# The causal mask of the first stage's attention, added by a product of identity and mask instead of by VectorE

## The reference

```
u = x @ w_in[l]                       # 1024 -> 7168 columns: conv, dq, dk, dv, mq, mk, mv, gates
y_a = conv_branch(...)                # depthwise causal convolution of 31 taps, layer norm, silu
# differential attention, 4 heads of two score matrices each:
s = einsum("qd,kd->qk", q, k) * scale
s = where(key_pos <= query_pos, s, -1e30)
p = softmax(s);  a = p[0] - lam * p[1];  o = a @ v
# moba attention, 8 heads: with 256 tokens and blocks of 256, plain causal attention
s = where(kpos <= qpos, s, -1e30);  p = softmax(s);  o = p @ v
m = gates[0] * y_a + gates[1] * y_b + gates[2] * y_c
x = layer_norm(ALPHA * x + m @ w_o[l])
h = relu(x @ w_ff1[l] + b)**2
x = layer_norm(ALPHA * x + h @ w_ff2[l] + b)
```

## Time and profile before

| | |
|---|---|
| time, median of 3 runs | 1386.25 us (1384.93 to 1388.49) |
| the profiled execution | 1385.95 us, span 1384.2 us |
| mean granted clock of TensorE | 0.975 |
| TensorE busy | 1293.9 us (93%), 8713 products |
| VectorE busy | 905.2 us (65%) |
| ScalarE busy | 586.5 us (42%) |
| mask adds (line 1216) | 32, of 428 ns each (median), from 85.2 to 650.8 us |
| score products (line 1903) | 64 in 128 passes of 272 to 480 ns, from 83.5 us on |

### The profile page before, as it was taken

How to read it: one execution, slowest core, us unless ns; L and a number is a source line. 1 busy time by engine, 2 the same in 40 slices (tenths; PEclk the granted TensorE clock), 3 DMA queues, 4 the chain that set the end, 5 groups by cost and what they waited for, 6 DMA issues and landing times.

```text
span 1384.2 us, 21687 instructions
## 1 busy us (share of the span) xinstructions
PE 1293.9 (93%) x8713; PEld 1096.8 (79%) x8713; DVE 905.2 (65%) x1464; ACT 586.5 (42%) x911; POOL 59.8 (4%) x84
## 2 busy tenths in 40 slices
PE   7999999989999899999898999969979979999996
PEld 6999888878888799999887888859878866555553
DVE  3999876876555789996587665684885573232223
ACT  3345674444444434566444444444535343111111
POOL 1000000000000000000000000020043000010100
PEclk9999999999999999999999999989999999999999
DMA  9754434565555456443355555555535576999994
GB/s 281 246 189 153 153 92 127 179 213 182 182 188 200 135 181 221 127 158 105 112 203 183 190 197 188 183 163 164 152 109 171 214 280 251 421 421 421 421 421 196
DMA packets 172583, 289.70 MB, mean 209 GB/s; under 512 B 10388, under 2 KB 143140, under 8 KB 160204
## 3 DMA queue, kind: packets, MB, share of 16 engines
q1 hardware_dynamic: 169580, 281.55, 58.1%
q0 software_dynamic: 2752, 6.82, 1.7%
q10 hardware_dynamic: 160, 0.08, 0.0%
HBM read 287.36 MB, written 3.16 MB: 210 GB/s over the span
## 4 chain that ended last, share of the span: by engine, by line
PE 64%; DVE 24%; ACT 5%; issue 3%; DMA 3%; SPq 1%; POOL 0%; DVEq 0%; ACTq 0%; POOLq 0%
PE ps L1775 11%; PE ps L1777 10%; PE ps L1776 10%; DVE w_lo L1144 8%; PE ps L1826 8%; PE ps L2272 7%; DVE cvh L1259 5%; ACT w_hi L737 4%; PE ps L1828 3%; PE ps L2304 3%; DMA raw<-in_w_up 2%; PE ps L2315 2%; DVE nm L1217 1%; DVE gT L1184 1%; DVE x_nat L1190 1%
## 5 line engine op out<-in xcount | busy, mean ns | idle before, releaser
L1144 DVE TENSOR_TENSOR w_lo<-raw,w_hi 128x2048 fp32r<-128x2048 f32 (+1 forms) x165 | 369.6, 2240 | 147.0 <-ACT w_hi L737 146.8
L737 ACT ACTIVATE w_hi<-raw 128x2048 fp32r<-128x2048 f32 (+1 forms) x165 | 307.4, 1863 | 244.6 <-PE ps L1777 229.4
L1775 PE MATMUL ps<-xT_both,w_lo 128*128 128x256 f32 x680 | 198.2, 292 | 0.0
L1776 PE MATMUL ps<-xT_both,w_hi 128*128 128x256 f32 x680 | 193.3, 284 | 0.0
L1777 PE MATMUL ps<-xT_both,w_hi 128*128 128x256 f32 x680 | 193.1, 284 | 0.0
L1826 PE MATMUL ps<-xT_both,w_hi 128*128 128x512 f32 x496 | 175.7, 399 | 0.0
L1775 PE MATMUL ps<-w_hi,xT_both 128*128 128x256 f32 (+2 forms) x536 | 162.0, 302 | 1.9 <-DVE w_lo L1144 1.7
L1776 PE MATMUL ps<-w_lo,xT_both 128*128 128x256 f32 (+2 forms) x536 | 159.1, 297 | 0.0
L1777 PE MATMUL ps<-w_hi,xT_both 128*128 128x256 f32 (+2 forms) x536 | 159.1, 297 | 0.0
L1775 PEld LDWEIGHTS ps<-xT_both,w_lo 128*128 128x128 f32 x680 | 131.3, 193 | 3.0 <-issue 2.7
L1776 PEld LDWEIGHTS ps<-xT_both,w_hi 128*128 128x128 f32 x680 | 131.5, 193 | 0.2
(11 more groups left out here) (410 smaller groups left out, 2273.0 us busy)
## 6 DMA issues: line engine op xcount, KB each, us to landing
raw<-in_w_in SPq DMA_DIRECT2D x72, 1024.0 KB, 5.2
raw<-in_w_ff SPq DMA_DIRECT2D x64, 1024.0 KB, 5.3
raw<-in_w_down SPq DMA_DIRECT2D x10, 1024.0 KB, 15.6
raw<-in_w_up SPq DMA_DIRECT2D x10, 1024.0 KB, 17.1
w_exp<-in_w_down SPq DMA_DIRECT2D x10, 1024.0 KB, 17.2
raw<-in_w_o SPq DMA_DIRECT2D x8, 1024.0 KB, 4.9
w_exp<-in_w_gate SPq DMA_DIRECT2D x8, 1024.0 KB, 16.5
raw<-in_w_gate SPq DMA_DIRECT2D x8, 1024.0 KB, 17.4
```

What stands on the lines that cost most here:

```text
L737: nc.scalar.activation(split_of(u)[0][:, 0:n], raw[:, u % RAW, 0:n], ACT.Copy).then_inc(hi_done, 1)
L1144: nc.vector.tensor_tensor(split_of(u)[1][:, 0:n], raw[:, u % RAW, 0:n], split_of(u)[0][:, 0:n].bitcast(F32), ALU.subtract).then_inc(split_ ...
L1775: nc.tensor.matmul(out_, left[1], right[0], start=start, stop=False)
L1776: nc.tensor.matmul(out_, left[0], right[1], start=False, stop=False)
```

## The change

The mask add of VectorE and its link are taken out. In its place the TensorE, behind the two score products, multiplies the identity with the mask into the diagonal block of both score banks, and adds it there to what the score products left (`start=False`). Both operands are fp32r copies of 128 x 128, which VectorE makes once, in unit 4 of layer 0, in parts of `rank` that are free until the routing. `score_done` is given by the last of the new products.

```diff
         ones_r, later_r, member_r = rank[:, 0:P], rank[:, P:2 * P], rank[:, 2 * P:].rearrange("p (a e) -> p a e", a=TT)
+        ident_r, mask_r = ones_r, later_r
...
                         dve.wait_ge(bcast_in, BCASTS)
+                        dve.wait_ge(ident_in, 16)
+                        nc.vector.tensor_scalar(ident_r, ident[:], 1.0, None, ALU.mult)
+                        nc.vector.tensor_scalar(mask_r, mask[:], 1.0, None, ALU.mult)
...
                         nk = P * (s % 2 + 1)
-                        diag = score[:, :, nk - P:nk]
-                        link(nc.vector.tensor_tensor(diag, diag, bc(mask[:], 1, 2), ALU.add))
                         nc.vector.tensor_reduce(nm[:, s % 2, :], score[:, :, 0:nk], AX.X, ALU.max, negate=True).then_inc(neg_max, 1)
...
                     for i in range(2):
                         part = slice(i * HD, (i + 1) * HD)
-                        last = nc.tensor.matmul(score[:, i, 0:nk], qkT[part, kind, c, a * P:(a + 1) * P], qkT[part, kind + 1, c, 0:nk], start=True, stop=True)
+                        nc.tensor.matmul(score[:, i, 0:nk], qkT[part, kind, c, a * P:(a + 1) * P], qkT[part, kind + 1, c, 0:nk], start=True, stop=False)
+                    for i in range(2):
+                        last = nc.tensor.matmul(score[:, i, nk - P:nk], ident_r, mask_r, start=False, stop=True)
                     last.then_inc(score_done, 1)
```

## The result

The changed kernel takes 1390.9 us (median of 9 executions), the one before 1386.33 us (median of 9): ratio 1.0027, interval 1.0017 to 1.0038, so 3.7 us slower (2.4 to 5.3); the two medians themselves lie 4.6 us apart, inside that interval. One of the nine executions of the changed kernel took 4445.65 us, for a reason that nothing here shows, and the ratio is taken without it. The forecast was 1388.2 us, within 0.3% of before; the time lies inside the range, 2 to 3 us above the forecast. The profiled execution took 1389.6 us, its span is 1387.7 us.

The account below looks back on a forecast made before the run. The prediction took the TensorE, full but for 4.8 us of stall, to bound the attention. Its terms, +7.0 - 4.8 - 0.6 + 0.4 = +2.0 us, gave 1388.2 us, range 1384.3 to 1392.5 us.

Parts of the forecast that it names:

- The TensorE is the bound, not VectorE of the chain: In both layers' attention the TensorE, almost without air, bounds; the rival, VectorE as bound, gave 1378.9 us, chance 4%.
- The stalls, -4.8 us: TensorE waits at line 1912, tasks 3 to 10, 2.4 us in layer 0; all gone in both layers, -4.8 us.
- The price of a pair, 0.25 us: Two fp32r identity-mask products behind a task's scores on the TensorE: 0.25 us, 28 times, +7.0 us.
- The bounds of 0.15 and 0.40: Pair prices in us of two rivals: cheap pair, 1385.5 us, chance 7%; dear pair, 1392.5 us, chance 22%.
- Tasks 14 and 15: Last two tasks of each layer: their mask products fall into 1.62 us of TensorE air and cost nothing.
- The relief, 0.3 us: Unit 25, last task of each layer: without the mask add VectorE's split starts 0.3 us earlier; twice, -0.6 us.
- The copies, +0.4 us: Two 128 x 128 copies by VectorE in unit 4 of layer 0, without cover: +0.4 us.
- What the profile would show: Signs: line 1912 waits gone, VectorE waiting for scores in most tasks, 14 us less busy, task 13 transposes 1.1 us later.

## Why the prediction was right, and where it was not

*The TensorE is the bound, not VectorE of the chain.* Right, and shown from three sides: without any mask only 2.6 us of 95.8 go, not 4.6; with both masks the pitch is that of the change; the wait of line 1912 for VectorE is gone in both.

*The stalls, -4.8 us.* They are 2.60 + 2.53 = 5.1 us. But the reason given is one of two, each of which is enough. I let VectorE's lead remove them, and without any mask it does; the kernel with both masks shows that the pairs' own 0.24 us, added up over the tasks, outrun them without any lead. Where one engine meets another only at a few late points, work put on the one that waits first fills the wait.

*The price of a pair, 0.25 us.* Measured 0.24, between the row of 200 columns (0.22) and that of the transposes (0.29). The bounds of 0.15 and 0.40, which made the range, were far too careful on the upper side.

*Tasks 14 and 15.* A step that failed. I counted the pair of task 14 as free because it stood "behind the unit that starts this path"; it stands ahead of unit 25, whose end starts ScalarE's half of the split, and the path runs through that half. 15 pairs count in each layer, not 14. The relief, 0.3 us, was about right in size (0.24 to 0.26), and is used up by this.

*The copies, +0.4 us.* 0.25 us: the copies take 0.14 us each, not 0.2.

*What the profile would show.* Line 1216 gone, 64 products in pairs, no wait of line 1912, the wait of the third head shorter (1.62 to 1.12 us): right. The transposes behind the scores of task 13 start 0.8 us later against the scores of task 0, not 1.1. VectorE waits for the scores only in two tasks from 80 to 160 us, for 0.7 us together, and in layer 1 in six tasks, not in most. It has caught up all the same: from task 5 on the maximum starts within 0.3 us of the end of the scores, where the mask add had started 2.6 to 4.4 us behind them in tasks 4 to 10. What I left out is that VectorE is held at the split instead, by ScalarE's half (2.7 us in five tasks, above), and that half waits for the TensorE's unit (31.0 us), so the lead can't grow. VectorE is 11.6 us less busy, not 14.

*The missing term: +2.3 us at the end.* With the measured sizes the sum is 30 × 0.24 - 5.1 - 0.5 + 0.25 = +1.8 us. That this is so near the forecast 2.0 is partly luck: two pairs more and larger stalls, a cheaper copy and a smaller relief cancel. The rest has nothing to do with the attention or with any engine's work. It goes with 30 instructions fewer in VectorE's stream. The prediction named no rival of this kind. That the time still fell into the range is luck: the term is smaller than the range, which had been made for another cause.

That VectorE waits for its own code there is the reading that fits: it stands at a skipped loop, nothing in the profile releases it, and it hangs on the number of instructions ahead. It is argued and not shown: no view tells what the engine waits for, and where the boundary lies between 1434 and 1449 instructions was not tried.

## What to carry to other kernels

Before moving work from a busy engine, walk the receiving engine's own timeline, pitch by pitch, and add up its stalls: they are the whole gain, however long the other engine stands in the chain that ended last. Here 5 us of stall were to be had, 32 moved tasks of 0.24 us cost 7 us, and 8 moved at the right places cost 2.

Count the path's starting events, too: work that stands ahead of the event is on the path, even if its own result is not needed.

When a small change does not close to within a microsecond, compare the traces by marks far from the edit; the rest may be a wait that belongs to no engine's work, like the one here that a few instructions in idle time removed.

## What was new of the hardware

VectorE's wait at a skipped loop has two lengths here, 2.9 to 3.0 us with 1434 of its instructions in the profile and 0.6 to 0.7 us with 1449 to 1494. Fifteen or thirty clears of one cell in idle time at the start change it from the long one to the short one.

A product of 128 x 128 by 128 columns in fp32r costs the TensorE 0.11 to 0.12 us with its load of weights (half of the 0.23 to 0.24 us of a pair), between float32 work on both sides as well, which is no less than one of 200 columns (0.11 us).
